# Sixteen attention units: turning by a product with diagonals made on GpSimd, and values taken for two units at once

## The reference, cut to what matters

```python
def windowed_gqa_sink_attention(q, k, v, sink, pos, is_real):
    ...
    mask = kreal[None, :] & (jnp.abs(qpos[:, None] - kpos[None, :]) <= WINDOW)
    s_band = jnp.einsum('bqhgd,bkhd->bhgqk', qi, kb).astype(jnp.float32) * scale
    s_band = jnp.where(mask, s_band, NEG_INF_2)
    s_meta = jnp.einsum('bqhgd,bmhd->bhgqm', qi, k_meta).astype(jnp.float32) * scale
    s_sink = jnp.broadcast_to(sink_g[None, :, :, None, None], s_meta.shape[:-1] + (1,))
    p = jax.nn.softmax(jnp.concatenate([s_band, s_meta, s_sink], axis=-1), axis=-1)
    ...
    return (jnp.einsum('bhgqk,bkhd->bqhgd', p_band, vb)
            + jnp.einsum('bhgqm,bmhd->bqhgd', p_meta, v_meta))
```

## Time and profile before

| | |
|---|---|
| median of 3 runs | 869.05 us (868.91 to 869.34) |
| the profiled execution | 870.0 us, span of the profile 868.2 us |
| TensorE busy | 858.9 us, 99% |
| VectorE busy | 626.8 us, 72% |
| ScalarE busy | 478.7 us, 55% |
| GpSimd busy | 68.9 us, 8% |
| the changed units in the span | from 465 us (scores of unit 0) to 555 us (values of unit 15) |

### The profile page before, as it was taken

How to read it: one execution, slowest core, us unless ns; L and a number is a source line. 1 busy time by engine, 2 the same in 40 slices (tenths; PEclk the granted TensorE clock), 3 DMA queues, 4 the chain that set the end, 5 groups by cost and what they waited for, 6 DMA issues and landing times.

```text
span 868.2 us, 13077 instructions
## 1 busy us (share of the span) xinstructions
PE 858.9 (99%) x4812; PEld 736.2 (85%) x4812; DVE 626.8 (72%) x985; ACT 478.7 (55%) x769; POOL 68.9 (8%) x96
## 2 busy tenths in 40 slices
PE   8999999999999999999999999999999999999997
PEld 6887788888888888889999888888888888888885
DVE  6867677666876666677688887887766876666665
ACT  6546633434644444446687887676653654444443
POOL 1000000000200000002122010132300100000000
PEclk9999999999999999999999999999999999999999
DMA  8955344554565555452766535745475365455531
GB/s 322 415 213 193 110 168 160 183 182 169 186 242 194 193 193 189 143 177 72 249 229 235 173 107 184 259 170 195 152 285 170 122 237 186 172 200 186 178 145 48
DMA packets 30334, 164.70 MB, mean 190 GB/s; under 512 B 3840, under 2 KB 5632, under 8 KB 12880
## 3 DMA queue, kind: packets, MB, share of 16 engines
q1 hardware_dynamic: 27840, 157.71, 51.1%
q10 hardware_dynamic: 2448, 6.37, 2.2%
HBM read 157.02 MB, written 3.83 MB: 185 GB/s over the span
## 4 chain that ended last, share of the span: by engine, by line
PE 97%; DVE 1%; DMA 1%; ACT 0%; issue 0%; SPq 0%; DVEq 0%; POOL 0%; ACTq 0%
PE ps L530 18%; PE ps L532 18%; PE ps L531 18%; PE ps L696 8%; PE ps L681 8%; PE ps L700 4%; PE ps L677 4%; PE ps L709 3%; PE ps L1802 2%; PE ps L711 2%; PE ps L565 1%; PE ps L1736 1%; PE ps L1760 1%; PE ps L1755 1%; PE ps L1750 1%; DMA raw<-weights 1%
## 5 line engine op out<-in xcount | busy, mean ns | idle before, releaser
L1901 DVE TENSOR_TENSOR wlo<-raw,whi 128x2048 fp32r<-128x2048 f32 x134 | 306.9, 2292 | 148.6 <-ACT whi L891 148.0
L891 ACT ACTIVATE whi<-raw 128x2048 fp32r<-128x2048 f32 x134 | 256.3, 1913 | 177.9 <-PE ps L532 108.5
L530 PE MATMUL ps<-whi,xT 128*128 128x512 f32 x192 | 76.8, 400 | 0.0
L532 PE MATMUL ps<-whi,xT 128*128 128x512 f32 x192 | 75.0, 391 | 0.0
L531 PE MATMUL ps<-wlo,xT 128*128 128x512 f32 x192 | 74.9, 390 | 0.0
L1371 POOL TENSOR_TENSOR stat<-stat,cst 128x1 f32<-128x1 f32 x10 | 11.9, 1201 | 489.2 <-DVE stat L1921 260.8
L530 PE MATMUL ps<-whi,fT_h 128*128 128x512 f32 x128 | 50.2, 392 | 0.0
L532 PE MATMUL ps<-whi,fT_l 128*128 128x512 f32 x128 | 49.8, 389 | 0.0
L531 PE MATMUL ps<-wlo,fT_h 128*128 128x512 f32 x128 | 49.8, 389 | 0.0
L530 PE MATMUL ps<-x_all,whi 128*128 128x272 f32 x160 | 46.4, 290 | 0.0
L532 PE MATMUL ps<-x_all,wlo 128*128 128x272 f32 x160 | 46.2, 289 | 0.0
(11 more groups left out here) (351 smaller groups left out, 1885.3 us busy)
## 6 DMA issues: line engine op xcount, KB each, us to landing
raw<-weights SPq DMA_DIRECT2D x134, 1024.0 KB, 4.8
kB<-key_parts SPq DMA_DIRECT2D x20, 272.0 KB, 3.3
key_parts<-knat SPq DMA_DIRECT2D x4, 544.0 KB, 3.0
cst<-consts SPq DMA_DIRECT2D x1, 1371.0 KB, 13.4
kswap<-kraw SPq DMA_DIRECT2D x8, 136.0 KB, 2.4
raw<-weights SPq DMA_DIRECT2D x4, 256.0 KB, 6.1
raw<-weights SPq DMA_DIRECT2D x2, 512.0 KB, 7.5
gate_a<-gain_rows ACTq DMA_DIRECT2D x2, 512.0 KB, 8.1
```

The source lines that it names most:

```text
L530: pe.matmul(o, lh, rh, start=first, stop=False)
L532: return pe.matmul(o, ll, rh, start=False, stop=last)
L891: act.activation(whi[s][:], raw[s][:], ACT.Copy).then_inc(split_hi, 1)
L1901: dve.tensor_tensor(wlo[s][:], raw[s][:], whi[s][:], ALU.subtract).then_inc(split_lo, 1)
```

## The change

For units 0 to 15 the exponentials are no longer scaled on ScalarE. GpSimd multiplies the identity by each head's reciprocals (`unit_diag`, two 128x128 operations a unit, signalled by `u_diag`), and TensorE turns the unscaled exponentials by an ordinary fp32 product with that diagonal in place of a transposition: exp^T x diag(1/sum) turns and scales. The narrow part becomes two products, one for each head's meta columns, 32 and 16 columns wide, at PSUM rows 0 and 32. Values are taken once for units 2n and 2n+1, with products 256 columns wide (`pair_values`), so `puT` and `pmT` hold two units, and `sT_h` and `sT_l` are made 256 columns at a time, one slot later. GpSimd's low parts of keys and queries are interleaved with the diagonals by slot. Where a slot has `values_out`, ScalarE's `queries_high` moves behind it. Some tiles get other places.

```diff
+            for q in range(2 * OUT2):
+                U = q - U0 - 1
+                if 0 <= U < S_UNITS:
+                    pool.wait_ge(u_pr, U + 1)
+                    if U >= 2:
+                        pool.wait_ge(u_pt, U - 1)
+                    for u in range(2):
+                        m = pool.tensor_scalar(unit_diag[:, U % 2, u, :], c("ident"), usoft[:, U % 4, 5, u:u + 1], None,
+                                               ALU.mult)
+                    m.then_inc(u_diag, 1)
+                if q % 2 == 1 and q // 2 - 2 in KEY_BLOBS:
+                    keys_rest(q // 2 - 2)
+                if q % 2 == 1 and q // 2 - 2 in QUERIES:
+                    queries_rest(q // 2 - 2)
...
-                U = q - U0 - 1
-                if 0 <= U < S_UNITS:
-                    act.wait_ge(u_pr, U + 1)
-                    for u in range(2):
-                        ins = act.activation(scores(U, u), scores(U, u), ACT.Copy, scale=usoft[:, U % 4, 5, u:u + 1])
-                    ins.then_inc(u_norm, 1)
...
             def unit_turn(U):
 
-                pe.wait_ge(u_norm if U < S_UNITS else u_pr, U + 1)
+                pe.wait_ge(u_diag if U < S_UNITS else u_pr, U + 1)
...
+                for u in range(2):
+                    for kt in range(NT):
+                        pe.matmul(ps[:, 6, (2 * u + kt) * P:(2 * u + kt + 1) * P], scores_of_tile(U, u, kt),
+                                  unit_diag[:, U % 2, u, :], start=True, stop=True)
+                for u, (a, b) in enumerate(((TOK, SECOND), (SECOND, SECOND + N_META))):
+                    m = pe.matmul(ps[a - TOK:b - TOK, 7, 32:32 + P], sc[U % 2][:, a:b], unit_diag[:, U % 2, u, :],
+                                  start=True, stop=True)
+                m.then_inc(u_pt, 1)
+
+            def pair_values(U):
+
+                pe.wait_ge(u_ptd, U + 2)
+                pe.wait_ge(u_ptm, U + 2)
+                result_read(U)
+                cc, _ = unit_place(U)
+                for u in range(2):
+                    a = (2 * (cc // 4) + u) * DH
+                    pe.matmul(ps[u * DH:(u + 1) * DH, 7, PAIR:PAIR + TOK], vs_meta[:, a:a + DH],
+                              pmT[:].rearrange("p a q -> p (a q)"), start=True, stop=False)
+                for kt in range(NT):
+                    for u in range(2):
+                        a = (2 * (cc // 4) + u) * DH
+                        m = pe.matmul(ps[u * DH:(u + 1) * DH, 7, PAIR:PAIR + TOK], vs[:, kt, a:a + DH],
+                                      puT[:, 2 * u + kt].rearrange("p a q -> p (a q)"), start=False, stop=kt == 1)
+                m.then_inc(u_o, 2)
...
-                if 0 <= U < S_UNITS:
-                    unit_values(U)
+                if 1 <= U < S_UNITS and U % 2 == 1:
+                    pair_values(U - 1)
...
-                    if U:
-                        dve.wait_ge(u_o, U)
+                    if U > 1:
+                        dve.wait_ge(u_o, U - U % 2 if U < S_UNITS else U - 1)
```

More of the change, by code:

```diff
@@ L46 @@
 XSTEP = 320
+PAIR = 160
 MIX1 = 2 + 1 + 2 + 2 + 4 + 4 + 4 + 4 + 2 + 4 + 4
@@ L312, in build @@
         rrow2 = at("rrow2", [P, TOK], F32, top[0])
-        ql = [new("ql0", [P, 2, TOK], F32R)]
+        top[0] += 2 * P
+        puT = new("puT", [P, 4, NT, P])
         assert top[0] <= 3 * BLOB
@@ L321, in build @@
         vb_meta = new("vb_meta", [P, D])
-        top[0] += 1536 - 960
+        ql = [new("ql0", [P, 2, TOK], F32R)]
+        top[0] += 1024 - 960
         dT_h = at("dT_h", [P, KC, TOK], F32R, top[0])
@@ L331, in build @@
         sc = [new("sc0", [P, SECOND + KEYS]), new("sc1", [P, SECOND + KEYS])]
-        puT = new("puT", [P, 4, P])
-        pmT = new("pmT", [P, P])
+        pmT = new("pmT", [P, NT, P])
+        unit_diag = new("unit_diag", [P, 2, 2, P])
         scratch2 = new("scratch2", [P, 2 * DH])
@@ L456, in build @@
         u_pr = sem("u_pr")
-        u_norm = sem("u_norm")
+        u_diag = sem("u_diag")
         u_pt = sem("u_pt")
@@ L1195, in _ @@
                     values_out(VALUES_AT[q])
+                    if m - 3 in QUERIES:
+                        queries_high(m - 3)
                 if q == 14:
@@ L1211, in _ @@
                     act.wait_ge(u_pt, U + 1)
-                    if U:
-                        act.wait_ge(u_o, U)
+                    if U > 1:
+                        act.wait_ge(u_o, U - U % 2 if U < S_UNITS else U - 1)
                     rows_used = QUAD + N_META if U < S_UNITS else QUAD
-                    act.activation(pmT[0:rows_used, :], ps[0:rows_used, 7, 32:32 + P], ACT.Copy).then_inc(u_ptm, 1)
-                U = q - U0 - 3
-                if 0 <= U < S_UNITS:
-                    act.wait_ge(u_o, U + 1)
+                    act.activation(pmT[0:rows_used, U % 2, :], ps[0:rows_used, 7, 32:32 + P], ACT.Copy).then_inc(u_ptm, 1)
+                U = q - U0 - 4
+                if 0 <= U < S_UNITS and U % 2 == 0:
+                    act.wait_ge(u_o, U + 2)
                     if U == 0:
@@ L1221, in _ @@
                         act.wait_ge(kd_out[1], 16 * 2)
[L1222 to L1225, removed]
+                    cc, _ = unit_place(U)
+                    act.activation(sT_h[:, cc, :], ps[:, 7, PAIR:PAIR + TOK], ACT.Copy).then_inc(d_hi, 2)
+                U = q - U0 - 3
+                if S_UNITS <= U < UNITS:
                     act.wait_ge(u_o, U + 1)
@@ L1250, in _ @@
                     keys_high(m - 2)
-                if q % 2 == 1 and m - 2 in QUERIES:
+                if q % 2 == 1 and m - 2 in QUERIES and q + 1 not in VALUES_AT:
                     queries_high(m - 2)
@@ L1746, in unit_values @@
                 (cc, t), o = unit_place(U), ps[:, 7, 288:288 + P]
[L1747 to L1760 removed]
+                pe.matmul(o, pmT[:, t, :], vb_meta[:, cc * P:(cc + 1) * P], start=True, stop=False)
+                for kt in range(NT):
+                    m = pe.matmul(o, puT[:, kt, t, :], vb[:, kt, cc * P:(cc + 1) * P], start=False, stop=kt == 1)
                 m.then_inc(u_o, 1)
```

58 lines of the change are left out of this document (21 added, 37 removed).

## The result

The changed kernel took 878.63 us (median of 5 runs, 878.36 to 879.41) against 869.05 us: a ratio of 1.0107, 95% interval 1.0096 to 1.0118. The forecast was 879.4 us, range 875.0 to 884.0. The profiled execution has a span of 876.8 us, against 868.2.

The account below looks back on a forecast made before the run. The prediction took TensorE's own work as the bound, with no wait for ScalarE. Terms +7.3, +7.4, -3.0 and -1.3 sum to +10.4 us on the median 869.05, giving 879.4 us, range 875.0 to 884.0.

Parts of the forecast that it names:

- (a): Four large turns of each unit on TensorE become fp32 products, 0.223 us each for 0.108: +7.3 us.
- That rival: A product in the large turns takes four times a transposition, 0.43 us: some 893 us, chance 0.01.
- (b): Each unit's narrow transposition becomes two narrow products with changes of array form, 0.58 us for 0.11: +7.4 us.
- (d): In seven slots the values block directly follows the narrow products, saving one change of array form each: -1.3 us.
- the middle of my three cases: Change between two kinds of array parts costs one full-array change, so (d) is -1.3 us; other cases 0 and -2.5.
- The rival without a pause at the change: Narrow products need no change of array: (b) +1.7, (d) nothing, 875.0 us; lower end of the forecast's 0.90.
- (c): Values for two units at once on TensorE, eight blocks of 1.65 us for sixteen of 1.01: -3.0 us.
- The queries' move: Moving two queries_high behind values_out on ScalarE was to change nothing on TensorE.
- ScalarE's relief: ScalarE loses two activations a unit, 15.0 us in all, worth nothing because TensorE waited for none of them.
- The price of a diagonal: GpSimd's 128x128 operations take 0.61 us each, 1.22 a unit, leaving about 0.9 us of room in even units.
- The rival of late diagonals: GpSimd's diagonals take over 2.3 us and TensorE waits for u_diag: +10, about 889 us, chance 0.05.
- The rival that pairing pays: Each TensorE instruction costs one 0.108 us slot, making (a) 0 and (c) -8.1: 867.0 us, chance 0.02.

Follow-up runs that it names:

- e3: Changed kernel with one full-array product of 128 columns in place of the two narrow products (second head's meta columns wrongly scaled): 875.38 us, 1.0062 of before.
- e4: Changed kernel turning by transpositions, diagonals made and waited for but unused, so the result lacks the scaling: 865.86 us, 0.9954 of before.
- e9: Changed kernel with two ScalarE activations per unit put back as copies of the scores onto themselves, and the turn waiting for them: 878.94 us, 1.0112 of before.
- e1: Kernel before with the pairing of values alone; ScalarE scales, TensorE transposes, queries at their old place: 869.21 us, 0.9994 of before.
- e8: Kernel before with pairs, late queries_high and both heads' scaling done in place on GpSimd, turns by transposition: 866.69 us, 0.9966 of before.
- e5: Changed kernel with every GpSimd diagonal made two or four times: 880.40 us (1.0130 of before) with two, 904.72 us (1.0408) with four.
- e2: Changed kernel without the pairing, products kept and values taken unit by unit: 879.91 us, 1.0116 of before.

## Why the prediction was right

- **(a) The large turns, +7.3.** The eight records run at 0.112 each, 0.89 us to the fifth product in e3, as forecast. The Trainium skill ("TensorE: Matmul & The Clock Gate", Terms) has transposition mode 4 times faster for FP32; the trace disagrees, the factor is 0.223/0.108, about 2.1, and no time near 893 us came out. That rival is out.
- **(b) and (d), +7.4 and -1.3.** The mechanism was right and the size a little high. The block without values came to 1.93 for 1.97, with values 3.38 for 3.44. e3's 3.6 us is the part of it that the changes of array form make. 505.61 to 505.94 holds two pairs of narrow records and the change to the 64-column arrays: from single starts 0.12 and 0.20 us, and the step back to full arrays is 0.20 too. So a change between two kinds of parts costs as much as one to the full array, the middle of my three cases. The two narrow products start 7 ns apart, as I had counted. The rival without a pause at the change, 875.0 us, is ruled out by this and by e3. The Trainium skill ("TensorEngine Tiling (Array Packing)", Key Properties) says that every change of mode drains the engine, and the trace agrees as far as it shows a pause at each change, 0.20 us from start to start in place of 0.11 to 0.12.
- **(c) The pairs, -3.0.** e4 gives -2.9 in a stream without waits, once the two pauses are taken off. The pair of 256-column records runs at 0.21 us, and the block behind the narrow products took 507.39 - 505.94 = 1.45, where 1.65 - 0.18 = 1.47 was forecast.
- **The queries' move, put at nothing.** It was worth -0.46: before had two pauses of TensorE for ScalarE's copy behind the queries' high parts, and the prediction, which found no slot stretched and no wait for ScalarE, had overlooked them. It is the move and not ScalarE's relief: in e9, with ScalarE loaded again, the distances at both places are the changed kernel's, 7.45 us from the first scores to the first turn and 5.38 from unit 5's turn to unit 6's.
- **Sum.** (a), (b) and (d) together are 13.4 by the prediction and 12.6 by the runs (changed kernel less e4); (c) -3.0 and -2.9; the queries' move 0 and -0.46. So 10.4 became 9.2 on the stretch and 9.6 on the medians, all within the range. The two misses, 0.8 in (b) and (d) and 0.46 here, go the same way, so the sum is not right because errors cancelled.
- **ScalarE's relief at nothing.** Right for this kernel, and e9 shows it. The reason I gave, that TensorE waited for none of it, was true of the scaling in before's slots, the two small pauses apart. e1 shows that the argument does not carry over to a kernel with shorter ones: had the change been the pairs alone, the sum would have said -3.0, and the chip gave -0.6.
- **GpSimd.** The price of a diagonal was right (0.602 for 0.61). The room was 1.64 us in the tightest unit and not the 0.9 counted in before's slots: ScalarE's high parts, and VectorE's subtraction behind them, come earlier without the scaling. e9, with most of that work put back, has 1.00. No diagonal met such a subtraction. The rival of late diagonals needed more than that room: with two it begins, with four it stands at its full size, and dearer than I had priced it.
- **The rival that pairing pays.** It had 867.0 us on the ground that a product costs one slot of 0.108. (a) rules it out. The time itself can be had, in another way: e8 gets 866.7 by moving the scaling and leaving the transpositions.

## What to carry to other kernels

Where TensorE's stream is the bound, a factor folded into a transposition turns it into an fp32 product of twice the records (0.223 us for 0.108 here), and narrow products add a change of array form on each side; an idle GpSimd can do the scaling itself and leave the transposition alone (e8). Before comparing two kernels, look for what else they differ in: the late `queries_high` was worth 0.46 us here, about a sixth of what pairing gave. A saving on TensorE of a tenth of a microsecond per slot has to be checked against what is late next: price each neighbour's order (which copy stands ahead of which) for the shorter slot. Work moved to an idle GpSimd should be priced by its room in microseconds in the tightest slot and with VectorE's two-input operations beside it, not by its busy share.

## What the runs showed of the hardware that I had not expected

That VectorE and GpSimd hold each other up stood in the prediction. New to me was how much it can take, and that it can strike a very short operation that TensorE waits for. A subtraction of VectorE's with two inputs from SBUF made a 0.60 us operation of GpSimd last 2.71 (e5 with four diagonals). In the other direction, a tiny operation of VectorE's in the changed kernel, first VectorE, then GpSimd:

```profile
480.02 1.18 DVE L2137 SCALAR_TENSOR_TENSOR usoft<-usoft,negsink 128x2 f32<-128x2 f32 x1
481.24 0.16 DVE L2139 TENSOR_TENSOR usoft<-usoft,negsink 128x2 f32<-128x2 f32 x1
```

```profile
479.89 1.30 POOL L1413 TENSOR_TENSOR ql<-kswap,qs 128x512 fp32r<-128x512 f32 x1 [0.17 <-ACT qs L1158]
```

Two numbers per partition take 1.18 us, until GpSimd's 1.30 us operation is over at 481.19, and the next one of the same size takes 0.16. The Trainium skill ("GPSIMD Engine Reference", Key points) says that GpSimd shares its SBUF interfaces with VectorE and contends with its instructions that run in a two-port performance mode or read two inputs from SBUF; these rows, all of two inputs, agree. An operation of VectorE's with one input was held up as well, in e2: TENSOR_SCALAR on 128x2 at 560.18 took 1.22 us in place of 0.17, beside a low part of queries. In e1 such a hold-up, of 0.94 us, stood ahead of a wait of TensorE of 0.91.

The granted clock fell to 0.66 and 0.83 in windows of 10 us that hold or follow TensorE's waits of up to 3.0 us in e5 with four diagonals, and stayed at 1.00 from 515 to 525 us, in which TensorE was idle for 3.6 us. In the page of e1, with waits of 1.3 and 0.9 us, it stays in the top tenth in all forty slices. What decides it is left open.
